# A decoder step of two mixer layers on one core: Delta's output gate projected one round later, the gate product on four column groups, and ring loads issued behind the stage's own

## The reference

```python
x = _layer_norm(ALPHA * x + (1.0 + gate_f) * y, ln_g[0, 1], ln_b[0, 1])   # end of layer 0
h = x * (1.0 + scale_m) + shift_m                                         # start of layer 1
p = h @ w_in                                   # 1024 x (4096 conv, 2048 z, 16 a, 16 b)
qkv, buf_new = _causal_conv(p[..., :4096], buf, conv_w)
q, k, v = ...                                  # silu, norm, 8 q/k heads, 16 v heads
g = -exp(a_log) * softplus(a + dt_bias);  beta = sigmoid(b)
o, s = _gated_delta_chunked(q, k, v, g, beta, s0)
o = _rms_norm(o, norm_g) * silu(z)             # z: the output gate
y = o @ w_out
```

## Time and profile before

| what | value |
|---|---|
| runs of the kernel before | 2418.91 us median of 3 (2414.42 to 2424.68) |
| profiled execution | 2408.83 us, span 2407.0 us |
| PE busy in the span | 1984.3 us (82%) |
| DVE, ACT, POOL busy | 811.7, 385.5, 356.7 us |
| mean granted TensorE clock | 0.893 of 2.4 GHz |

### The profile page before, as it was taken

How to read it: one execution, slowest core, us unless ns; L and a number is a source line. 1 busy time by engine, 2 the same in 40 slices (tenths; PEclk the granted TensorE clock), 3 DMA queues, 4 the chain that set the end, 5 groups by cost and what they waited for, 6 DMA issues and landing times. The chain is left out here.

```text
span 2407.0 us, 33215 instructions
## 1 busy us (share of the span) xinstructions
PE 1984.3 (82%) x13493; PEld 1098.1 (46%) x13493; DVE 811.7 (34%) x1666; ACT 385.5 (16%) x872; POOL 356.7 (15%) x476
## 2 busy tenths in 40 slices
PE   5999999998896799737988898898986769759980
PEld 3443434333343444326655655655754634334430
DVE  0123233233423200053255535535535414320007
ACT  1000100000000111132132232232221100011110
POOL 0010101101022000122030031031021002300004
PEclk9999999999998799956998998998895889869995
DMA  9625344350602699793222113023034480159974
GB/s 334 226 83 204 125 146 167 114 175 34 253 40 81 223 350 348 277 347 104 70 85 77 58 52 112 19 85 97 30 113 142 153 255 35 40 183 343 343 258 166
DMA packets 221242, 381.86 MB, mean 159 GB/s; under 512 B 17165, under 2 KB 88469, under 8 KB 221078
## 3 DMA queue, kind: packets, MB, share of 16 engines
q1 hardware_dynamic: 214002, 354.22, 42.3%
q0 software_dynamic: 7104, 25.69, 2.8%
HBM read 305.25 MB, written 74.63 MB: 158 GB/s over the span
## 5 line engine op out<-in xcount | busy, mean ns | idle before, releaser
L545 PE MATMUL bank<-ring,hT 128*128 128x512 f32 x768 | 345.1, 600 | 3.1 <-PEq L262 2.0
L1272 PE MATMUL bank<-hT,ring 128*128 128x272 f32 x1024 | 309.8, 438 | 1.3 <-PEq L879 1.3
L2213 PE MATMUL bank<-ring,exp_xT 128*128 128x512 f32 x512 | 232.8, 608 | 18.3 <-issue 14.6
L545 PEld LDWEIGHTS bank<-ring,hT 128*128 128x128 f32 x768 | 142.3, 191 | 188.3 <-issue 185.6
L1272 PEld LDWEIGHTS bank<-hT,ring 128*128 128x128 f32 x1024 | 196.4, 207 | 56.0 <-issue 21.2
L2791 PE MATMUL bank<-ring,oT 128*128 128x512 f32 x384 | 175.3, 618 | 13.2 <-DMA oT<-oT_spill 12.6
L2213 PEld LDWEIGHTS bank<-ring,exp_xT 128*128 128x128 f32 x512 | 96.8, 194 | 134.9 <-issue 129.9
L2791 PEld LDWEIGHTS bank<-ring,oT 128*128 128x128 f32 x384 | 75.7, 199 | 108.2 <-issue 95.2
L2232 PE MATMUL bank<-ring,exp_aT 128*128 128x512 f32 x256 | 115.4, 593 | 1.6 <-ACT exp_aT L2267 1.6
L1269 PE MATMUL bank<-ring,hT 128*128 128x512 f32 x256 | 112.9, 602 | 0.0
L2302 DVE TENSOR_TENSOR exp_a<-bank,exp_sg 128x256 f32<-128x256 f32 x32 | 13.6, 425 | 278.1 <-ACT exp_sg L2285 278.1
(11 more groups left out here) (437 smaller groups left out, 2535.1 us busy)
## 6 DMA issues: line engine op xcount, KB each, us to landing
ring<-in_moe_w_gu_dram SPq DMA_DIRECT2D x32, 2048.0 KB, 9.3
ring<-in_w_ada_dram SPq DMA_DIRECT2D x24, 2048.0 KB, 9.5
ring<-in_moe_w_down_dram SPq DMA_DIRECT2D x32, 1024.0 KB, 11.6
ring<-in_ret_w_in_dram SPq DMA_DIRECT2D x8, 2048.0 KB, 13.5
ret_Ss<-in_state_ret_dram SPq DMA_DIRECT2D x32, 512.0 KB, 5.1
out_dram<-ret_Ss SPq DMA_DIRECT2D x32, 512.0 KB, 3.9
expert_outputs<-exp_y SPq DMA_DIRECT2D x32, 512.0 KB, 4.7
ring<-in_dn_w_in_dram SPq DMA_DIRECT2D x8, 2048.0 KB, 9.1
```

The lines of the kernel that those rows point to most:

```text
L545: last = pe.matmul(ps[u % 2][:, :], core.hT[:, k, tok(t)], core.ring[:, w % RING, k, :], start=(k == 0), stop=(k == KD - 1))
L1272: mm = pe.matmul(ps[U % 2][:, 0:HALF], core.ring[:, w % RING, k, c * P:(c + 1) * P], core.hT[:, k, half * HALF:(half + 1) * HALF], start=( ...
L2213: last = pe.matmul(ps[v][:, :], xT[:, v, k, :], wgu[v][:, k, :], start=(k == 0), stop=(k == KD - 1))
```

## The change

In `combine_features`, x tiles 1 to 4 are loaded behind the norm's rows and only when the gathers of tile 0 are there; the `w_ada` blocks follow the gathers of tile 1, not 2; the modulations 13, 14 and 15 stand ahead of tiles 2, 3 and 4; the first three delta blocks are no longer fetched here. In `delta_gates` these blocks are fetched behind the stage's own loads; a and b are made transposed, with `wab` stationary on four column groups, copied to SBUF, and folded and turned back by five matmuls; all five tiles of x2 are made by DVE, between its other steps, and all are stored at the end. In `delta` the five z units of a group move to the round of its own steps: two at the head, alone, and three merged with the steps; in the last round these three take the first quarter of the list and `LAST` the part from 0.3 to 0.98.

```diff
@@ delta_gates
+        abT = st.sb("abT", [P, NTOK])
...
-                for t in (0, 3, 1, 4, 2):
+                for t in range(NT):
                     sp.dma_start(xn[0:rows(t), t, :], d["xn"](t)).then_inc(xn_in[t], 16)
-                for n, t in enumerate(by_dve):
-                    sp.wait_ge(s["xb_dve"], n + 1)
-                    sp.dma_start(d["x2"](t), xn[0:rows(t), t, :]).then_inc(s["x2_out"], 16)
+                core.load(sp, core.mix[1][0] + RING - 1)
                 sp.wait_ge(s["rows_kept"], 2)
...
-                for n, t in enumerate(by_pool):
-                    sp.wait_ge(s["xb_pool"], n + 1)
+                for t in range(NT):
+                    sp.wait_ge(s["offset_done"], t + 1)
                     sp.dma_start(d["x2"](t), xn[0:rows(t), t, :]).then_inc(s["x2_out"], 16)
...
-                for n, t in enumerate(by_pool):
-                    affine(pool, t, "xg_pool", "xb_pool", n + 1)
...
                 pe.wait_ge(s["wab_in"], 16)
+                for cols, out in ((slice(0, SEQ), ps[6]), (slice(SEQ, NTOK), ps[7])):
+                    for k in range(KD):
+                        j = k % 4
+                        last = pe.matmul(out[NS * j:NS * (j + 1), 0:cols.stop - cols.start], wab[:, k, :], core.hT[:, k, cols],
+                                         start=(k < 4), stop=(k >= 4), skip_group_check=True)
+                    last.then_inc(s["abT_done"], 1)
+                pe.wait_ge(s["abT_kept"], 2)
                 for i in range(NT):
-                    for k in range(KD):
-                        last = pe.matmul(ps[0][0:rows(i), i * 32:(i + 1) * 32], core.hT[:, k, tok(i)], wab[:, k, :],
-                                         start=(k == 0), stop=(k == KD - 1))
+                    last = pe.matmul(ps[0][0:rows(i), i * 32:(i + 1) * 32], abT[:, tok(i)], core.fold[:, 0:NS],
+                                     start=True, stop=True)
...
+                act.activation(abT[:, 0:SEQ], ps[6][:, :], ACT.Copy).then_inc(s["abT_kept"], 1)
+                act.activation(abT[:, SEQ:NTOK], ps[7][:, 0:NS], ACT.Copy).then_inc(s["abT_kept"], 1)
...
-                for n, tile in enumerate(by_dve):
-                    affine(dve, tile, "xg_dve", "xb_dve", n + 1)
...
                 dve.wait_ge(s["x_done"], 1)
+                affine(0)
+                affine(1)
                 dve.wait_ge(s["lned"], 1)
...
+                affine(2)
                 dve.wait_ge(s["sums_done"], 2)
...
+                affine(3)
+                affine(4)
@@ delta
+        HEAD = 2
...
+            first = [0] + [UN * g + 16 for g in range(G)] + [UN * G]
             for g in range(G + 1):
-                steps = group(g - 1) if g else []
...
+                mm = [("mm", U, k) for U in range(first[g], first[g + 1]) for k in range(KD)]
+                if g == 0:
+                    yield from mm
+                elif g < G:
+                    yield from mm[:HEAD * KD]
+                    yield from merge(group(g - 1), mm[HEAD * KD:])
+                else:
+                    yield from mm[:HEAD * KD]
+                    rest = mm[HEAD * KD:]
+                    yield from merge(group(g - 1), rest, LAST, at={1: [0.25 * (i + 0.5) / len(rest) for i in range(len(rest))],
+                                                                   2: [0.3 + 0.68 * (i + 0.5) / len(LAST) for i in range(len(LAST))]})
@@ combine_features
-                for t in range(1, NT):
-                    sp.dma_start(x[0:rows(t), t, :], x_from(t)).then_inc(x_in[t], 16)
...
-                sp.wait_ge(got[2], 32)
+                sp.wait_ge(got[0], 32)
+                for t in range(1, NT):
+                    sp.dma_start(x[0:rows(t), t, :], x_from(t)).then_inc(x_in[t], 16)
+                sp.wait_ge(got[1], 32)
                 core.load(sp, core.ada_w[15])
...
-                core.load(sp, core.mix[1][0] + RING - 1)
...
-                    if t == 3:
-                        core.modulate(pe, 13, ps[4])
+                    if t >= 2:
+                        core.modulate(pe, 11 + t, ps[2 + t])
...
-                for n in (14, 15):
-                    core.modulate(pe, n, ps[n - 9])
```

More of the change, by code:

```diff
@@ L861, in delta_gates @@
         xn, gain, offset = st.sb("xn", [P, NT, D]), st.sb("gain", [P, D]), st.sb("offset", [P, D])
-        by_dve = (0, 1, 2)
-        by_pool = (3, 4)
         s = {n: st.sem(n) for n in ("ins", "wab_in", "conv_in", "zeroed", "ab_done", "ab_kept", "x_done", "absd", "exped", "lned", "aled",
                                     "beta_done", "steps", "g_done", "sums_done", "dif_done", "out_done", "rows_done",
-                                    "rows_kept", "rows_out", "smp_ps", "smp_kept", "conv_ps", "conv_kept", "norm_in", "xg_dve",
-                                    "xg_pool", "xb_dve", "xb_pool", "x2_out")}
+                                    "rows_kept", "rows_out", "smp_ps", "smp_kept", "conv_ps", "conv_kept", "norm_in", "gained",
+                                    "offset_done", "x2_out", "abT_done", "abT_kept")}
         xn_in = [st.sem(f"xn_in{t}") for t in range(NT)]
[L870 to L877, removed]
         with nc.Block() as block:
@@ L956, in _ @@
             def _(act):
+                act.wait_ge(s["abT_done"], 1)
+                act.activation(abT[:, 0:SEQ], ps[6][:, :], ACT.Copy).then_inc(s["abT_kept"], 1)
+                act.wait_ge(s["abT_done"], 2)
+                act.activation(abT[:, SEQ:NTOK], ps[7][:, 0:NS], ACT.Copy).then_inc(s["abT_kept"], 1)
                 act.wait_ge(s["ab_done"], 1)
@@ L993, in _, with affine @@
                 chain(dve.memset(t.kdec[:], 0.0))
-                for n, tile in enumerate(by_dve):
-                    affine(dve, tile, "xg_dve", "xb_dve", n + 1)
+                def affine(i):
+                    row = xn[0:rows(i), i, :]
+                    dve.wait_ge(s["norm_in"], 32)
+                    dve.wait_ge(xn_in[i], 16)
+                    dve.tensor_tensor(row, row, gain[0:rows(i), :], ALU.mult).then_inc(s["gained"], 1)
+                    dve.wait_ge(s["gained"], i + 1)
+                    dve.tensor_tensor(row, row, offset[0:rows(i), :], ALU.add).then_inc(s["offset_done"], 1)
                 dve.wait_ge(s["ins"], total)
@@ L1119, in group @@
             return out + merge(b_steps(2 * g + 1), c[:10]) + c[10:]
+        HEAD = 2
         LAST = [("AM", n, part) for n in range(16, 24) for part in range(4)]
         def schedule():
+            first = [0] + [UN * g + 16 for g in range(G)] + [UN * G]
             for g in range(G + 1):
-                steps = group(g - 1) if g else []
-                if g == G:
-                    steps = merge(steps, LAST)
-                mm = [("mm", UN * g + u, k) for u in range(UN) for k in range(KD)] if g < G else []
-                tail = 5 * KD if steps else len(mm)
-                yield from merge(steps, mm[:len(mm) - tail]) if steps and mm else steps
-                yield from mm[len(mm) - tail:] if mm else []
+                mm = [("mm", U, k) for U in range(first[g], first[g + 1]) for k in range(KD)]
[9 more added lines that the diff above has]
+                                                                   2: [0.3 + 0.68 * (i + 0.5) / len(LAST) for i in range(len(LAST))]})
         def unit(U):
```

## The result

The changed kernel takes 2334.57 us (median of 4, 2329.23 to 2342.6) against 2417.89 for the kernel before: ratio 0.9655, 95% interval 0.9619 to 0.9691. The forecast was 2376 with a range from 2350 to 2402. Timed again, the ratio was 0.9661 (0.9631 to 0.9691).

What follows compares the result with a forecast made beforehand. Bounds: transfers and DVE's chain in combine_features, chains of waits in delta_gates, PE gaps on DVE results in delta. Terms -6.5, -15.6 and -20 sum to -42.1 us from 2418.91, giving 2376, range 2350 to 2402.

Steps and rivals of the forecast that it cites:

- A fifth more filler takes about 0.25 us from each, 3 us; I take 4 in all: Delta rounds 1 to 3: denser filler shortens about a dozen PE waits, 4 us each round, 12 for three.
- One more microsecond for the clock: Delta: denser work holds up PE's clock, worth 1 us within delta's -20.
- Rival 2: Delta: the clock rises under denser work, delta -43 us, time 2354; chance 0.15.
- The last round: Delta's last round: 15.8 us of z work enters its first quarter, about 7 us saved; grows from 148.3 by about 9.
- Combine_features: Seam stage: earlier gathers for tile 0 (3 us) and earlier modulations (3.5 us), together -6.5 us.
- Delta_gates: Gates' stage: earlier wab, faster product and shorter DVE waits, but transfers end it at about 37 us: -15.6 us.
- the first half of the Trainium skill's sentence: Delta_gates: DMA engines consume descriptors in ring order, so loads delay the x2 stores and the stage takes 37 us.
- the other half: Delta_gates: a later descriptor may finish its write before an earlier one; stage nearer 31 us, sum 6 us better.
- (1): Delta: PE's gaps stay because DVE chains simply start later, delta gains nothing, time 2397; chance 0.2.
- (3): Seam gains half: combine_features at 0 and gates at -10, time 2389; chance 0.15.
- (4): Delta's merged rounds slow as their clock falls from 0.88 to 0.74, 26 us a round, time 2475; chance 0.03.
- (5): Whole change does not do what it says: an unseen transfer sets stage and round ends, time 2419; chance 0.02.

Runs made afterwards that it cites:

- the run with empty places: Kernel before, old order, with a merged stretch's 128 channel items in the last 128 of 152 places, no work added: rounds of 187.5 us against 192.3.
- the repeats: Kernel before and changed kernel each traced again, unaltered: mean rounds of 192.3 us (six rounds) before and 173.0 us (nine rounds) changed.
- the three runs with later blocks: Changed kernel with two, or only the last, of three delta blocks behind the x2 stores, two runs with further edits: ratios 0.9692, 0.9635, 0.9736 to the kernel before.
- The run with early idle columns: Kernel before with 240 more unread columns in first halves of the first three channels, rounds 1 to 3: rounds of 193.2 us against 192.3.
- The closer packing: Changed kernel with z items of rounds 1 to 3 in the list's first 0.10, not 0.16, and third delta block behind x2 stores: ratio 0.9736.

## Why the prediction was wrong

**The step that failed** is "A fifth more filler takes about 0.25 us from each, 3 us; I take 4 in all". I summed the listed waits and asked how much more filler stood directly ahead of each. The idle time fell by 10.6 us in place of 4. The waits do not shrink by a little each: single ones of 3.7, 3.0 and 2.2 us went or were halved. Of the 10.6 us, 4.6 come without any added work, from the shift of the channel units towards the end (the run with empty places), a term that the working did not have. **The second** is "One more microsecond for the clock": it was 10 us of PE's time in each of three stretches. Both terms belong to rounds 1 to 3, which won 19.3 us each by the repeats and not 4. These rounds were forecast at 12 us in all, plus the one for the clock, and came to 58.

**The ranges** failed with them. I gave delta a bound of -45 and capped each round at 10. But the whole of the moved work could be hidden, 15.8 us in each of four rounds, 63 us, and the earlier trace rows allowed it: 27 us idle and 40 us at the lower clock stood beside 15.8 us of work. Rival 2, with 0.15, had the right mechanism for rounds 1 to 3 and half its size, 5 us each. Its other half, in the last round, did not come: the clock there went from 0.74 to 0.77. The sign that it was right, a clock moved by over 0.05 in the merged stretches, was there (0.06 to 0.07).

**The last round** was right: 148.3 to 158.2 us where the working gave 157.1. Of the 5.9 us saved, 4.9 are idle time and 1.0 the clock (0.74 to 0.77). The gap of 3.0 us before L1428 went, as said. The wait of 4.8 us before L1361 stayed (4.9 us, now L1375), where 1 to 2 us were to come off, so the closeness of the total is in part luck.

**Combine_features** won 4.1 us in the first trace and 4.2 to 7.7 in the other traces with its code (48.0 to 51.5 us), for -6.5. Tile 0 had its gathers 9.3 us after the stage's start in place of 11.2, 1.8 us sooner where 3 were forecast. The last tile was ready 1.8 us sooner too, but waited for modulation 15: its block landed 41.9 us after the start, with 39.7 forecast, and the modulation took 3.51 us and not 2.7. The recorded reading of the earlier trace rows was wrong here. The last block's issue before began at 1032.80, not at about 1037, so it had landed at 1053.5 and not at 1057.5, 41.1 us after the stage's start. The change brought it no sooner.

The last block's issue by SP in the kernel before, and its landing in the changed one, where the issue began at 1038.20:

```profile
1032.80 5.64 SPq L140 DMA_DIRECT2D ring<-in_w_ada_dram  x1
```

```profile
ring<-in_w_ada_dram SPq DMA_DIRECT2D x1, 2048.0 KB, 24.3
```

SP's timeline and PE's waits in the changed stage, and a window over these loads:

```profile
1032.50 14.57 SPq L140 DMA_DIRECT2D ring<-in_w_ada_dram  x3
```

```profile
PE bank L184 <- DMA ring<-in_w_ada_dram: 4.8, 3, 2.3
```

```profile
1037.00:1062.00 25.00, 12.23 (x160) 10.16 (x160) 21.57 (x26) 11.88 (x16) 13.03 (x15) 0.62 1.04 358
```

SP needed 14.57 us to issue the three loads that took 6.71 before. But the DMA engines were full all the while (share 1.04), so the slow issue is not shown to be what made the blocks late.

**Delta_gates** gave -11.6 for -15.6. `wab` was there 2.45 us after the stage's start (PE's first matmul is at 1074.69), with 2 to 4 forecast; the product, 3.85 us with its sample columns, had been put at 4.9; the affines ran at 1.22 us with POOL out of them. The transfers ended 4 us later than the 37 forecast, because they moved at 316 GB/s over the stage and not 365: the small loads at its start reached 228.

Windows of the changed stage: all, its first 10 us, the rest:

```profile
1072.20:1113.00 40.80, 17.75 (x138) 13.31 (x138) 14.26 (x22) 9.77 (x22) 0.00 (x0) 0.50 0.93 316
1072.20:1082.20 10.00, 6.92 (x51) 4.02 (x52) 0.62 (x4) 1.14 (x5) 0.00 (x0) 0.50 0.81 228
1082.20:1112.00 29.80, 10.84 (x89) 9.29 (x88) 13.65 (x18) 8.63 (x18) 0.00 (x0) 0.50 1.00 356
```

By the first half of the Trainium skill's sentence (DMA: Bandwidth & Descriptors, Queues, rings and completion order) the stores wait behind the loads; the 9.2 and 11.2 us here, and the 35 us of the three runs with later blocks, agree. The stage would have been nearer 31 by the other half, and was not.

**Rivals.** The gaps did not stay (1), the seam won most of its share (3), nothing was slower (4), and the change does what it says (5). On the clock, the Trainium skill (TensorE: Matmul & The Clock Gate, What's actually happening) says that activity releases the throttle. The run with early idle columns agrees: PE busy 36.88 of 40 us at 0.96, where the kernel before had 33.17 at 0.87. The first quarter of the last round, for which the prediction cited the sentence, did not stay at the upper level: 0.85 over its first 40 us, with PE busy 30.86 of them. Two other rows show that PE's busy share alone does not give the clock. The closer packing had PE busy 36.03 of 40 us at 0.79, and the kernel before ran 10 us at the lower level without a gap:

```profile
1281.50:1291.50 10.00, 10.00 (x81) 5.89 (x80) 5.89 (x20) 3.41 (x7) 0.77 (x1) 0.50 0.15 41
```

## What to carry to other kernels

Where PE shows both gaps and the lower clock, moving independent matmul work out of a stretch of its own into the latency-bound one can win its whole length. Bound the gain by the whole of the work moved plus what the displacement of other items can give (15.8 and about 5 us a round here), not by the filler ahead of the listed waits. Then try neighbouring places: the same three units cost 11 to 17 us more a round when packed closer or spread wider. Fetch ahead behind a stage's own loads. Blocks put behind the stores on which the stage ends shorten that stage, but the next stage's first small loads then stand behind them.

## What the runs showed of the hardware

Taking work away did not make rounds shorter: 6.8 us less a round gave 175.4 us where 173.0 had been, with the clock at 0.89 to 0.93 in place of 0.94 to 0.97. The clock's course is mostly the kernel's own: in 20 us windows of rounds 1 to 3 it repeated within 0.02 over most of two traces, and the runs with other places for the same work moved it. It is not wholly fixed: in one traced round of the changed kernel a window stood at 0.91 that had 0.57 in the two others, and the round took 167.8 and not 174.7 us. And issuing a transfer is not always cheap: with full DMA engines the three 2 MB loads of combine_features held SP for 14.57 us where it had been 6.71. Small loads behind ring blocks wait with them: 16 KB landed in 8.5 us behind two blocks, and in 2.1 us without.
